# A transformer's last output projection as three fp32r products, with its operands split on ScalarE, GpSimd and VectorE

## The reference

```python
h = rmsnorm(x, norm_g[l]);  z = h @ w_in[l]                  # 1024 -> 3328
o_a, o_b, o_c, o_d = dense, window, neighbourhood, differential attention of parts of z
o_d = rmsnorm(o_d, subln_d[l]) * (1.0 - lam_init)
mix = concat([o_a * silu(g_a), o_b * silu(g_b), o_c * silu(g_c), o_d * silu(g_d)])
x = x + mix @ w_out[l]                                       # 1024 -> 1024
```

## Time and profile before

| what | us |
|---|---|
| median of 3 runs (lowest, highest) | 1169.44 (1168.6, 1170.05) |
| the profiled execution's own time | 1169.03 |
| its span, first to last instruction | 1167.2 |
| TensorE busy | 1136.5 |
| VectorE busy | 744.3 |
| ScalarE busy | 505.2 |
| GpSimd busy | 55.5 |
| mean granted clock of TensorE | 0.998 |

### The profile page before, as it was taken

One profiled execution on the slowest core, in us unless ns is written; L12 is line 12 of the kernel. 1 busy time (PEld: TensorE's weight loads), 2 busy tenths in 40 slices (PEclk: granted clock), 3 DMA queues, 4 the chain that ended last, 5 costly groups with the idle time before them and its releaser, 6 DMA issues. The chain is left out here.

```text
span 1167.2 us, 21650 instructions
## 1 busy us (share of the span) xinstructions
PE 1136.5 (97%) x9272; PEld 1018.4 (87%) x9272; DVE 744.3 (64%) x1090; ACT 505.2 (43%) x716; POOL 55.5 (5%) x47
## 2 busy tenths in 40 slices
PE   5999999999999999999999999999999999999997
PEld 4789998899999998799998899999997777877776
DVE  5587665736665565787675556555667675567744
ACT  5355442234333344455442143333355655446642
POOL 1002000000000000011000000000002100030000
PEclk9999999999999999999999999999999999999999
DMA  9543334454454355443335345434436334353310
GB/s 350 224 161 109 122 111 161 188 201 159 182 216 174 152 195 188 147 142 109 120 106 227 124 187 217 197 147 195 180 139 227 108 109 181 112 219 132 130 65 37
DMA packets 27465, 188.15 MB, mean 161 GB/s; under 512 B 3456, under 2 KB 4352, under 8 KB 5504
## 3 DMA queue, kind: packets, MB, share of 16 engines
q1 hardware_dynamic: 25808, 175.89, 40.8%
q10 hardware_dynamic: 1440, 8.55, 1.9%
q0 software_dynamic: 144, 2.66, 0.6%
HBM read 181.84 MB, written 5.24 MB: 160 GB/s over the span
## 5 line engine op out<-in xcount | busy, mean ns | idle before, releaser
L650 PE MATMUL bank<-in_low,h_high 128*128 128x512 f32 x352 | 138.4, 393 | 0.0
L650 PE MATMUL bank<-in_high,h_high 128*128 128x512 f32 x288 | 117.2, 407 | 13.4 <-DVE in_low L1932 12.1
L1069 PE MATMUL bank<-h_high,gate_split 128*128 128x256 f32 x704 | 129.1, 281 | 0.2
L1069 PE MATMUL bank<-h_high,up_split 128*128 128x256 f32 x704 | 128.6, 280 | 0.0
L1085 PE MATMUL bank<-act_split,down_split 128*128 128x256 f32 x960 | 118.4, 283 | 0.0
L1085 PEld LDWEIGHTS bank<-act_split,down_split 128*128 128x128 f32 x960 | 116.6, 192 | 0.0
L675 PE MATMUL bank<-h_high,in_high 128*128 128x256 f32 x384 | 115.7, 301 | 0.5 <-DVE in_low L1806 0.5
L1357 ACT ACTIVATE in_high<-ring 128x2048 fp32r<-128x2048 f32 x47 | 89.6, 1910 | 55.3 <-PE bank L650 54.7
L650 PE MATMUL bank<-in_high,x_low 128*128 128x512 f32 x288 | 113.3, 393 | 0.0
L1069 PEld LDWEIGHTS bank<-h_high,gate_split 128*128 128x128 f32 x704 | 109.9, 189 | 0.9 <-DVE h_low L1748 0.6
L1069 PEld LDWEIGHTS bank<-h_high,up_split 128*128 128x128 f32 x704 | 109.8, 189 | 0.0
(11 more groups left out here) (339 smaller groups left out, 2252.4 us busy)
## 6 DMA issues: line engine op xcount, KB each, us to landing
ring<-w_in_dram SPq DMA_DIRECT2D x72, 1024.0 KB, 4.9
ring<-w_gate_up_dram SPq DMA_DIRECT2D x44, 1024.0 KB, 7.4
ring<-w_down_dram SPq DMA_DIRECT2D x22, 1024.0 KB, 4.8
ring<-w_out_dram SPq DMA_DIRECT2D x16, 1024.0 KB, 6.0
ring<-p_all_dram SPq DMA_DIRECT2D x6, 1024.0 KB, 4.8
x_kept<-scratch ACTq DMA_DIRECT2D x4, 1024.0 KB, 4.6
x<-x_kept ACTq DMA_DIRECT2D x4, 1024.0 KB, 7.8
table<-tables_dram POOLq DMA_DIRECT2D x1, 2594.0 KB, 12.2
```

The source lines that it names most:

```text
L650: last = mm(bank[(n - n % 2 + t) % 4][:], a, b, start=c == 0 and i == 0, stop=c == KT - 1 and i == 2)
L1069: last = mm(bank[2 * half + part][:, f * S:(f + 1) * S], a, b, start=k == 0 and i == 0, stop=k == KT - 1 and i == 2)
```

## The change

1. Each output-projection product becomes three in fp32r: weights high by mix high, high by mix low, low by mix high. In piece 32 the low part of the last mix comes behind the four high products of each block.
2. ScalarE copies the four weight tiles to fp32r (`out_high(q)`) into two buffers used in turn, so q = 2 waits for the end of piece 27 and q = 3 for that of piece 29. GpSimd subtracts for q = 0, 1 and 3 (two instructions of 128x1024 each), VectorE for q = 2 (`out_low`), back into the ring's slot.
3. ScalarE copies mixT[0..2] to fp32r (`mixed_high`), VectorE subtracts (`mixed_low`); for the last, ScalarE copies the turned y straight to fp32r and VectorE makes the low part from PSUM.
4. In `attend`, the gate is turned directly behind piece p instead of behind weigh(1) and piece p+2; VectorE makes the gate ahead of the scaling, and ScalarE copies it behind exps(1).
5. In the last attention two blocks of piece 30 move ahead of weigh(3) and two more ahead of values(3), and two blocks of piece 31 behind the turning of y; the halves of layer 1's first two tiles are subtracted later.

The diff, cut to its core:

```diff
+        o2_high = [nc.alloc_sbuf_tensor_at(f"out2_high{q}", [P, 2, D], F32R, offset=scratch_at + 4 * (4608 + 2048 * q)) for q in range(2)]
+        o2_low = [nc.alloc_sbuf_tensor_at(f"out2_low{q}", [P, 2, D], F32R, offset=ring_at + 8192 * SLOT2[G2 + q]) for q in range(4)]
...
+                    if q == 2:
+                        pe.wait_ge(*o2_lo_v.after(l, k + 1))
+                    elif k == 0:
+                        pe.wait_ge(*o2_lo_p.after(l, (1, 2, None, 3)[q]))
...
                     if q == 3:
                         if k == 1:
                             return
-                        for m in range(KT):
-                            for k in range(2):
-                                last = mm(bank[m // 2][:, m % 2 * S:(m % 2 + 1) * S], w[:, k, m * P:(m + 1) * P], mixT[q][:, k, :],
-                                          start=False, stop=m % 2 == 1 and k == 1)
-                            if m % 2:
-                                last.then_inc(wo2_end.sem, 1)
+                        for m0 in range(0, KT, 2):
+                            for m in (m0, m0 + 1):
+                                for k in range(2):
+                                    for a in range(2):
+                                        part(m, k, a, 0)
+                            if m0 == 0:
+                                pe.wait_ge(*mx_lo.after(l, 4))
+                            for m in (m0, m0 + 1):
+                                for k in range(2):
+                                    last = part(m, k, 0, 1, m == m0 + 1 and k == 1)
+                            last.then_inc(wo2_end.sem, 1)
                         return
+                    pe.wait_ge(*mx_lo.after(l, q + 1))
                     for m in blocks:
-                        last = mm(bank[m // 2][:, m % 2 * S:(m % 2 + 1) * S], w[:, k, m * P:(m + 1) * P], mixT[q][:, k, :],
-                                  start=False, stop=False)
-                    if k == 1:
+                        for a, b in ((0, 0), (0, 1), (1, 0)):
+                            last = part(m, k, a, b)
+                    if k == 1 and KT - 1 in blocks:
                         last.then_inc(wo2.sem, 1)
...
                     piece(l, p)
+                    y_transposes(l, n, b_eg_t, b_mix, n + 1, b_mtp, bank[6])
                     piece(l, p + 1)
+                    pe.wait_ge(*b_gT.after(l, n + 1))
                     weigh(0)
                     scores(2, 3)
                     weigh(1)
                     piece(l, p + 2)
-                    pe.wait_ge(*att.pt.after(l, 4 * n + 2))
-                    y_transposes(l, n, b_eg_t, b_mix, n + 1, b_mtp, bank[6])
                     values(0)
-                    pe.wait_ge(*b_gT.after(l, n + 1))
                     weigh(2)
...
                 values(2)
+                piece(l, 30, range(2))
                 weigh(3)
-                piece(l, 30, range(2))
+                piece(l, 30, range(2, 4))
                 values(3)
-                piece(l, 30, range(2, KT))
-                piece(l, 31)
+                piece(l, 30, range(4, KT))
+                piece(l, 31, range(6))
                 y_transposes(l, 3, a_y, b_mix, 4, b_mtp, bank[7])
-                pe.wait_ge(*b_mT.after(l, 4))
+                piece(l, 31, range(6, KT))
+                pe.wait_ge(*mx_hi.after(l, 4))
...
+                act.wait_ge(*wo2.after(l, 2))
+                out_high(3)
                 exps(6)
                 exps(7)
                 copy(2)
...
-                attention(l, att, 8, 4, 1, lambda n: bias[:, :, n, :], splits={1: split_gate(12, 3, 2304)})
+                attention(l, att, 8, 4, 1, lambda n: bias[:, :, n, :], between={1: lambda: gate_ready(l, 3, 2304)},
+                          splits={1: lambda l: (in_split2(l, 12), mixed_low(1))})
...
+                attention(l, att, 12, 8, 2, None, splits={1: lambda l: mixed_low(2), 3: lambda l: next_half(0, 0), 5: lambda l: out_low(2, 1)},
+                          mixing={5: lambda l: out_low(2, 0), 7: lambda l: next_half(0, 1)})
...
+                for n, q in enumerate((0, 1, 3)):
+                    pool.wait_ge(*o2_hi.after(l, q + 1))
+                    for k in range(2):
+                        last = nc.gpsimd.tensor_tensor(o2_low[q][:, k], ring[:, SLOT2[G2 + q], k * D:(k + 1) * D],
+                                                       o2_high[q % 2][:, k].bitcast(F32), ALU.subtract)
+                    last.then_inc(o2_lo_p.sem, 1)
                 pool.wait_ge(*b_dss.after(l, 1))
```

More of the change, by code:

```diff
@@ L1644, in _, with out_high, mixed_high @@
                 turned(l, 0, 256, qs)
+                def out_high(q):
+                    s = SLOT2[G2 + q]
+                    act.wait_ge(*ring_in2[s].after(l, SLOT2[:G2 + q].count(s) + 1))
+                    f(o2_high[q % 2][:], ring[:, s, :].rearrange("p (k n) -> p k n", k=2), ACT.Copy).then_inc(o2_hi.sem, 1)
+                def mixed_high(n):
+                    act.wait_ge(*b_mT.after(l, n + 1))
+                    f(mix_high[n][:], mixT[n], ACT.Copy).then_inc(mx_hi.sem, 1)
                 def gate_copy(n):
@@ L1671, in _ @@
                 exps(1)
+                gate_copy(1)
+                mixed_high(0)
                 next_high(l, 7)
@@ L1685, in _ @@
                 gate_sigmoid(l, 2304)
+                act.wait_ge(*bias_ok.after(l, 2))
+                out_high(0)
                 exps, copy = attention(l, att, 8, 8, 1, lambda n: a_s[:, n % 2, :])
@@ L1689, in _ @@
                 exps(1)
+                gate_copy(2)
+                mixed_high(1)
                 copy(0)
@@ L1698, in _ @@
                 turned(l, 6, 256, 32 ** -0.5)
+                out_high(1)
                 act.wait_ge(*b_full.after(l, G2))
@@ L1711, in _ @@
                     in_split2(l + 1, 0)
+                act.wait_ge(*wo2.after(l, 1))
+                out_high(2)
                 exps(4)
@@ L2323, in gated_turned, with mixed_low, out_low @@
                     tt(mixT[n], bank[7][:].rearrange("p (k s) -> p k s", k=2), gT, ALU.mult).then_inc(b_mT.sem, 1)
+                def mixed_low(n):
+                    dve.wait_ge(*mx_hi.after(l, n + 1))
+                    tt(mix_low[n][:], mixT[n], mix_high[n][:].bitcast(F32), ALU.subtract).then_inc(mx_lo.sem, 1)
+                def out_low(q, k):
+                    dve.wait_ge(*o2_hi.after(l, q + 1))
+                    tt(o2_low[q][:, k], ring[:, SLOT2[G2 + q], k * D:(k + 1) * D], o2_high[q % 2][:, k].bitcast(F32), ALU.subtract)\
+                        .then_inc(o2_lo_v.sem, 1)
                 def gated():
@@ L2393, in _ @@
                 gated()
+                dve.wait_ge(*mx_hi.after(l, 4))
+                stt(mix_low[3][:], bank[7][:].rearrange("p (k s) -> p k s", k=2), 0.5, mix_high[3][:].bitcast(F32), ALU.mult, ALU.subtract)\
+                    .then_inc(mx_lo.sem, 1)
                 dve.wait_ge(*x_back2.after(l, 1))
```

46 lines of the change are left out of this document (27 added, 19 removed).

## The result

| | us |
|---|---|
| kernel before, median of 5 runs beside the change | 1169.44 (1168.33 to 1170.05) |
| changed kernel, median of 5 runs | 1180.96 (1180.50 to 1183.32) |
| ratio, 95% interval | 1.0106 (1.0095 to 1.0117) |
| profiled execution of the changed kernel: its time, its span | 1183.32, 1181.5 |

The change costs 11.5 us, where the forecast's sum had 12.8.

What follows compares the result with a forecast made beforehand. TensorE's queue plus its waits was taken as the bound. Last stage 3.5 + 3.65, attention 2 4.8, attention 1 0.55, attention 0 0.3 sum to +12.8 on 1169.4: 1182 us, range 1170.5 to 1187.

Steps and rivals of the forecast that it cites:

- Products: Output projection on TensorE: three fp32r products replace each fp32 one, pieces fall from 3.46 to about 3.0 us, -4.0 a layer.
- ScalarE's fourth copy: Last attention: the copy waits for piece 29 ahead of exps(6), so TensorE idles 4.5 us at values(2) in each layer.
- GpSimd beside mix_pair(3): Last attention: GpSimd's subtraction holds off VectorE's mix_pair(3), so TensorE waits at weigh(3), +2.1 us a layer.
- the upper bound of the hold-off: A two-input VectorE operation waits for one whole GpSimd instruction, 2.4 us, the upper of the bounds 0 and 2.4.
- From values(3) to the end: End of last attention: y ready 6.2 us behind values(3), 1.6 wait at its turning; stage +3.65 in layer 1, +3.5 in layer 0.
- Attention 2, +2.4 a layer: Attention 2: GpSimd's out_low(0) holds back the gate by 0.6, then normed, the split and mixed_low by 2.3; +2.4 a layer.
- The gates: Gate turned one step earlier: attention 0 +0.15, attention 1 +0.1 and +0.45 by layer, attention 2 -0.25 without GpSimd.
- The clock: TensorE's clock may fall behind the 4.5 us idle time, 1.5 to 2 us a layer on top; left out of the sum, chance 0.13.
- between: Whole kernel: a result between the forecast and the harmless-GpSimd case, 1174 to 1179 us; chance 0.12.
- GpSimd harmless: Rival: GpSimd's subtractions hold nobody up in attention 2, attention 0 or the last stage; +2.1, 1171.5 us, chance 0.15.
- The clock falls: Rival: TensorE drops to half pace behind the 4.5 us idle time at values(2), 1185 us in all; chance 0.13.
- faster: Rival: copy(2) isn't late at values(2) and weigh(3) doesn't wait, so the change gains; -6, 1163 us, chance 0.1.

Runs made afterwards that it cites:

- e7_moved: Changed kernel, all arithmetic kept: out_high(3) behind copy(2), out_high(0) and out_low(0) behind attention 2's copy(2), out_low(3) on VectorE, next weights' halves later; 1165.28 us.
- e1_high3_late: Changed kernel with ScalarE's out_high(3) and its wait for piece 29 moved behind copy(2); 1174.55 us.
- e2_filler: Changed kernel with 18 products of a zero matrix on TensorE between piece 29 and values(2); 1182.15 us.
- e4_small_gpsimd: Changed kernel with GpSimd subtracting only 8 columns each time; products of tiles 0, 1 and 3 use the weights' high part instead of the low; 1176.20 us.
- e3_gates_only: Kernel before with only the new order of the gates, no products in parts, copies or subtractions; 1168.94 us, ratio 1.0000.
- e6_small_filler: e4_small_gpsimd plus the 18 filling products of e2_filler ahead of values(2); 1173.39 us.
- e5_late_small: Changed kernel with the edits of e1_high3_late and e4_small_gpsimd together; 1164.74 us, ratio 0.9962.
- e9_half_behind: e7_moved with VectorE's half split next_half(1, 0) moved behind the low part of the mixed y, layer 0 only; 1163.67 us.

## Why the prediction was right, and where it was not

The forecast was 1182, the result 1180.96. Point by point:

- *Products.* A piece takes 2.9 to 3.2 us (3.0 forecast). Their -4.0 a layer can be seen only where the faults are gone: -2.1 and -2.8 in the last stages of e7_moved, after the waits that I had named.
- *ScalarE's fourth copy.* Forecast 4.5 us of idle time at values(2), measured 4.31 in layer 1; values(2) at t = 25.0 against 25.3. e1_high3_late shows the cause.
- *GpSimd beside mix_pair(3).* Forecast +2.1; the scalings are 2.0 us longer, and e2_filler shows the wait of 2.00 that follows with the values at full clock. In the changed kernel only 0.44 and 0.62 us of it show as a wait, since TensorE itself was slow on the way there, and in layer 1's stage GpSimd costs 1.07. To take the upper bound of the hold-off was right, for scalings and for operations on two tensors.
- *From values(3) to the end.* Forecast 6.2 us from values(3) to y and a wait of 1.6. Layer 1: 6.7 with 1.57, where 0.4 of it is the clock. Layer 0: 7.2 with 2.36, of which 0.8 is GpSimd's first step held off by the half split. That was missed: I had put the halves in "VectorE's idle time" at no cost, and forgot that the rule works in both directions.
- *Attention 2, +2.4 a layer.* Too high: it came to +1.33 and +1.34. By e4_small_gpsimd GpSimd costs 1.58 and 1.27 there, and by e3_gates_only the order of the gates gives back 0.26 and 0.25. The step that failed is the count of what is held off. I charged 0.6 at the gate, and 2.3 behind it. In layer 1 the gate (L2359) took 0.78 instead of 0.69 (in layer 0 1.17), and only the first scalings (L1897) were late:

```profile
1105.21 0.78 DVE L2359 SCALAR_TENSOR_TENSOR scratch<-scratch,arena 128x512 f32<-128x512 f32 x1
...
1106.15 2.51 DVE L1897 TENSOR_SCALAR scratch<-scratch,stats 128x256 f32<-128x256 f32 x2
...
1103.05 5.19 POOL L2521 TENSOR_TENSOR out_low<-ring,out_high 128x1024 fp32r<-128x1024 f32 x2 [43.89 <-ACT out_high L1675]
```

  Read one by one, GpSimd's two instructions run from 1103.05 for 2.39 us and from 1105.40 for 2.85, the second 0.5 longer than the 2.33 that one takes undisturbed. The gate, from 1105.21 to 1105.99, slips in between and holds the second off for those 0.5 us; the scalings then wait for its end. What is left is one delay of 1.9 us instead of 0.6 and 2.3 in a row.

  In layer 1 another 0.3 us of attention 2 comes from neither of these. The stage is 23.10 in e4_small_gpsimd and 22.77 in e7_moved, and VectorE's first mask addition (L1909) starts 1.58 us behind the first scores in the one and 1.23 in the other. What e7_moved has taken away from there is ScalarE's copy out_high(0), which I had costed at nothing. By which wait the copy acts no trace shows.
- *The gates.* Attention 1 +0.04 and +0.43, forecast +0.1 and +0.45; attention 2 without GpSimd -0.25, measured -0.26 and -0.25 in e3_gates_only. Attention 0 was forecast at +0.15 and came to -0.21 and -0.03. GpSimd's bias addition does meet the gate there: L2359 takes 1.92 and 1.97 us and ends 0.6 behind it (1059.72 and 1059.17 in layer 1). But TensorE waits only 0.23 and 0.32 us at the gate's turning, where I had 0.65.
- *The clock.* I gave its fall 0.13 and left it out of the sum. It happened, in both layers, and alone costs 2.3 us in layer 1 (I had said 1.5 to 2 a layer). The Trainium skill, "TensorE: Matmul & The Clock Gate", section "HAM oscillation — how this bites in real kernels", has it that waits between bursts of matmuls send the array back to 1.2 GHz, and the trace agrees: the clock column is at 0.50 behind the 4.31 us. I weighed the two sides as if nothing were known between 1.1 and 12.1 us, though the idle time was to be the longest but one of the whole kernel.

So the number came out well partly by luck. By the profiled execution the last stage of layer 1 was under-priced by 0.9 us and that of layer 0 by 2.8 (its 3.5 is 3.35 by its own terms), attention 2 over-priced by 2.1 over both layers, and attention 0 by 0.5. Within the last stage of layer 1 two errors partly cancelled: without GpSimd and without the clock it is 1.23 longer than before (e6_small_filler), where the forecast had 1.5; the clock adds 2.29, where the sum had nothing, and GpSimd 1.07, where it had 2.1. The sign and the main mechanism did not hang on this luck.

Of the rivals, "between" fell with the result. "GpSimd harmless" fell with e4_small_gpsimd, and its price was wrong too: with GpSimd's work shrunk the kernel takes 1176.2 and not 1171.5, and 2.8 of these 4.7 us are the clock (e6_small_filler). "The clock falls" came true in its mechanism; its 1185 was too high, as GpSimd costs less beside it. The "faster" one described its own condition rightly, since with copy(2) not late and weigh(3) not waiting (e5_late_small) the time is 1164.7, where I had worked out 1163.

## What to carry to other kernels

A copy that waits for a buffer belongs behind everything that the fast engine is about to need, even if the copy itself is due soon: look at what is queued behind the wait, not at how long the copy takes. Work given to GpSimd was free here only where VectorE read PSUM or idled, and small steps of GpSimd on a chain must be kept from VectorE's long ones too. An idle stretch of 4 us on TensorE should be priced at its own length and the slow matmuls behind it (here 2.3 us more), unless another wait follows that would hide them.

## What the runs showed that I had not expected

- At the turning of y in layer 0 the clock sometimes falls, sometimes not, and the length of the wait does not decide it. Behind a wait of 1.57 us it fell (e9_half_behind, profiled), behind one of 2.35 it stayed (e7_moved):

```profile
1003.00:1005.00 2.00, 1.58 (x12) 1.41 (x13) 1.76 (x3) 0.60 (x1) 0.00 (x0) 1.00 0.02 4
1005.00:1007.00 2.00, 2.00 (x11) 2.00 (x11) 2.00 (x3) 0.00 (x0) 0.00 (x0) 0.53 0.54 127
1007.00:1009.00 2.00, 2.00 (x13) 2.00 (x13) 1.29 (x2) 0.67 (x2) 0.00 (x0) 0.62 0.94 393
```

```profile
1004.00:1006.00 2.00, 1.04 (x9) 1.05 (x10) 1.93 (x3) 0.35 (x1) 0.00 (x0) 1.00 0.02 4
1006.00:1008.00 2.00, 2.00 (x17) 1.82 (x17) 1.75 (x3) 0.25 (x1) 0.00 (x0) 1.00 0.29 49
1008.00:1010.00 2.00, 2.00 (x19) 2.00 (x19) 1.34 (x3) 1.18 (x3) 0.00 (x0) 1.00 0.88 373
```

  The 54 matmuls behind the turning take 8.25 us in the one and 6.72 in the other, 1.5 us apart. The changed kernel's profiled execution had such a second fall in layer 0. In the kernels with the copy moved the spread goes with the clock: the runs of e7_moved with a mean clock of 0.998 take at most 1164.77 us and those with 0.997 at least 1165.28, and e5_late_small is parted likewise, at 1164.74 and 1165.81. The five runs of the changed kernel lie 2.8 us apart, and their mean clocks (0.990 at 1180.50 and at 1182.65, 0.991 at 1183.32) are in no such order, so what spreads them stays open.
- Useless products can shorten a kernel: 36 of them, 4.3 us a layer in TensorE's idle time, took 2.8 us off e4_small_gpsimd, and nothing off the changed kernel.
- Why the clock fell behind a wait of 2.00 us in e2_filler, right after the filling products, stays open. No run varied the length of a wait with all else equal.
